# A gather-and-table transformer layer: eight more row pairs among the branch products, fourteen fewer ahead of the dense keys' weights, six of them in the last phase

## What is computed

```
h = layer_norm(x)
z = h @ W_in + b_in                       # 6400 columns: Fourier | q,k,v | memory q | gates
y_a, y_b, y_c = fourier(z) @ W_a, dilated_attention(z) @ W_b, memory_attention(z, mem) @ W_c
merged = sum_i sigmoid(gate_i) * y_i
h = layer_norm(alpha * h + merged @ W_o)
q = h @ W_pq                              # 8 heads, two halves each
s1, s2 = q1 . sub_keys1, q2 . sub_keys2   # 128 scores each
v1, i1, v2, i2 = top 16 of s1, top 16 of s2
sc, experts = top 16 of the 256 sums, expert = 128 * i1 + i2
gate = softmax(sc)
y = sum over 8 heads x 16 experts of gate * gelu(u_tab[expert] . h) * v_tab[expert]
out = layer_norm(alpha * h + y)
```

## Time and profile before

| | us |
|---|---|
| median of 3 runs | 1882.39 (1881.47 to 1882.58) |
| the profiled execution | 1882.71 |
| its span | 1880.9 |
| TensorE busy | 1710.1 (91%) |
| VectorE busy | 1250.8 (67%) |
| ScalarE busy | 204.6 (11%) |
| POOL busy | 635.2 (34%) |
| mean DMA rate | 263 GB/s |

### The profile page before, as it was taken

The page is one execution under the profiler, slowest core; times in us unless marked ns, Lnnn a source line. Parts: engine busy times, 40 slices in busy tenths (PEclk is TensorE's granted clock), DMA queues, the critical chain, the costliest instruction groups (busy, mean ns, idle before and its releaser), DMA issues.

```text
span 1880.9 us, 19525 instructions
## 1 busy us (share of the span) xinstructions
PE 1710.1 (91%) x7236; PEld 1213.9 (65%) x7236; DVE 1250.8 (67%) x2616; ACT 204.6 (11%) x431; POOL 635.2 (34%) x536
## 2 busy tenths in 40 slices
PE   7999999989999799999728899999999958799996
PEld 6588878967555668888527666666666547544442
DVE  3343175122567669997888986777777699966664
ACT  1101033101111021112100000111011010000000
POOL 2000000000246200146550175765665661265340
PEclk9999999999999989999867799999999976799998
DMA  6715201954779635679992199999999991299994
GB/s 221 235 45 158 83 7 40 286 166 145 243 266 370 246 124 175 217 261 409 388 356 62 51 400 409 409 409 409 397 409 409 409 372 61 77 404 410 409 403 151
DMA packets 193834, 493.81 MB, mean 263 GB/s; under 512 B 14103, under 2 KB 92952, under 8 KB 193444
## 3 DMA queue, kind: packets, MB, share of 16 engines
q0 software_dynamic: 74672, 271.55, 37.6%
q1 hardware_dynamic: 119068, 221.01, 33.1%
HBM read 489.32 MB, written 7.90 MB: 264 GB/s over the span
## 4 chain that ended last, share of the span: by engine, by line
PE 43%; DVE 26%; DMA 14%; POOL 9%; issue 7%; ACT 0%; SPq 0%; DVEq 0%
PE ps L639 42%; DMA arena<-in_v_tab_dram,experts 10%; POOL arena L604 5%; DVE arena L1336 5%; POOL arena L613 4%; DVE arena L1303 2%; DVE arena L1314 2%; DMA arena<-in_v_tab_dram 2%; DVE i L1233 2%; DVE pos L1248 1%; DVE arena L1302 1%; DVE v L1232 1%; DVE best L1247 1%; PE ps L651 1%; DMA arena<-in_w_mem_kv_dram 1%
## 5 line engine op out<-in xcount | busy, mean ns | idle before, releaser
L639 PE MATMUL ps<-arena 128*128 128x256 f32 (+4 forms) x6016 | 1503.1, 412 | 75.8 <-ACT arena L887 23.1
L639 PEld LDWEIGHTS ps<-arena 128*128 128x128 f32 (+1 forms) x6016 | 1035.9, 188 | 537.9 <-issue 285.9
L604 POOL DMA_INDIRECT arena<-in_u_tab_dram,experts x256 | 326.6, 1276 | 860.5 <-DVE dots L1314 531.6
L1336 DVE SCALAR_TENSOR_TENSOR arena<-arena,coef 128x1024 f32<-128x1024 f32 x254 | 327.3, 1289 | 111.0 <-DMA arena<-in_v_tab_dram,experts 110.2
L1314 DVE CUSTOM_DVE_ANT_0 arena<-arena 128x1024 f32<-128x1024 f32 x256 | 312.4, 1224 | 87.9 <-DMA arena<-in_u_tab_dram,experts 87.7
L613 POOL DMA_INDIRECT arena<-in_v_tab_dram,experts x256 | 297.3, 1161 | 148.3 <-DVE arena L1336 97.7
L887 ACT ACTIVATE arena<-ps 128x256 f32<-128x256 f32 (+2 forms) x212 | 88.9, 427 | 765.7 <-PE ps L639 722.0
L639 PE MATMUL ps<-hotg,arena 128*128 128x64 f16 x512 | 68.1, 303 | 26.8 <-DVE hotg L1304 25.5
L639 PEld LDWEIGHTS ps<-hotg,arena 128*128 128x128 f16 x512 | 59.9, 147 | 34.7 <-DVE hotg L1304 34.7
L1198 DVE TENSOR_TENSOR arena<-arena,ps 128x128 f32<-128x128 f32 (+1 forms) x32 | 13.4, 418 | 103.0 <-PE ps L639 91.7
L887 ACT ACTIVATE arena<-ps,bT 128x128 f32<-128x128 f32 (+2 forms) x68 | 36.6, 538 | 313.5 <-PE ps L639 313.5
(11 more groups left out here) (127 smaller groups left out, 793.3 us busy)
## 6 DMA issues: line engine op xcount, KB each, us to landing
arena<-in_u_cols_dram SPq DMA_DIRECT2D x128, 512.0 KB, 6.8
arena<-in_v_tab_dram SPq DMA_DIRECT2D x128, 512.0 KB, 6.8
arena<-in_w_in_dram SPq DMA_DIRECT2D x37, 1024.0 KB, 5.6
arena<-in_w_o_dram SPq DMA_DIRECT2D x8, 1024.0 KB, 9.9
arena<-in_w_pq_dram SPq DMA_DIRECT2D x8, 1024.0 KB, 5.4
beta_copies<-beta_rows SPq DMA_DIRECT2D x1, 4608.0 KB
arena<-in_w_mem_kv_dram SPq DMA_DIRECT2D x4, 1024.0 KB, 18.6
arena<-in_w_a_dram SPq DMA_DIRECT2D x8, 512.0 KB, 6.2
```

The costliest lines, as they stand in the source:

```text
L604: nc.gpsimd.indirect_dma_start(out=u_ring[:, n % ROWS, :], out_offset=None, in_=u_tab[0], in_offset=bass.IndirectOffsetOnAxis(ap=experts[: ...
L639: return nc.tensor.matmul(dst, lhsT, rhs, start=start, stop=stop, skip_group_check=True)
L1336: nc.vector.scalar_tensor_tensor(out=y_acc, in0=row, scalar=by, in1=y_acc, op0=ALU.mult, op1=ALU.add).then_inc(v_used, 1)
```

## The change

Two lines of constants change; V_PAIRS[1] follows from them and goes from 65 to 71.

```diff
-YO_PAIRS, TAIL_PAIRS = 36, 40
+YO_PAIRS, TAIL_PAIRS = 44, 48
 TOP_PAIRS = 8
-REST_PAIRS = 42
+REST_PAIRS = 28
 X_PAIRS = (4, 4)
 V_PAIRS = (118, PAIRS_IN - TAIL_PAIRS - TOP_PAIRS - REST_PAIRS - sum(X_PAIRS) - 118)
```

## The result

The changed kernel takes 1857.28 us (median of 4 runs, 1854.1 to 1860.1) against 1882.08 us before on the same chip: a ratio of 0.9868, 95% interval 0.9847 to 0.9889. Forecast were 1859.0 and a range of 1846 to 1872. Run once more beside other kernels it took 1855.16, a ratio of 0.9853 (0.9836 to 0.9869).

What follows compares the result with a forecast made beforehand. Bounds: TensorE in the tail and last phase, VectorE and its gathers ahead of the shares, VectorE at the first table phase's end. +10.6 - 46 + 0 + 7 + 5 = -23.4 us gave 1859.0 us, range 1846 to 1872.

Steps and rivals of the forecast that it cites:

- What bounds each stage: Second tail and last phase: TensorE; ahead of the shares: VectorE and its gathers; first table phase's end: TensorE waits for VectorE.
- Tail, +10.6: Second tail: three pairs and a head's key search before the last branch product start the output product 10.6 us later.
- crowded tail: Rival, second tail: rows wait, unit 22 is late, output product starts near 622; +8 more, 1867 us; chance 0.12.
- TensorE waiting for weights before 599: Second tail: sign that would show the prediction wrong; it took no wait for weights there.
- The clock: TensorE after the tail's wait: a 15 us wait costs the same 2 us or so as the present one; nothing added.
- 2 us more: TensorE at the shares: if the 33 us wait vanished wholly, the clock would give back some 2 us more.
- Ahead of the shares, -46: Before the dense keys' softmax shares: fourteen fewer pairs let VectorE reach them at 933 to 935, not 981.25; -46 us.
- 926: Dense keys on TensorE: key 59 could be emptied at 725.90 + 58 x 3.45 = 926.0, before the tail's delay.
- HBM rate: Ahead of the shares: measured 393 GB/s decides over the skill's about 358, which would leave the change worth about 4 us.
- Spreading phases, +10 and -10: Two spreading phases: one key search enters the first, another leaves the second; +10 and -10, together 0.
- First table phase, +7: First table phase: its last key search stands seven pairs before the end instead of thirteen; +7 us, bounds 0 and +8.3.
- Last phase, +5: Last phase: six more pairs at 4.03 us use up and overdraw VectorE's 18 us of cover; +5 us, bounds 0 and +9.

Runs made afterwards that it cites:

- tail_only: Against the kernel before: only YO_PAIRS, TAIL_PAIRS raised from 36, 40 to 44, 48, REST_PAIRS left at 42; 1899.54 us, ratio 1.0081.
- rest_only: Against the kernel before: only REST_PAIRS cut from 42 to 28, tail as before, all fourteen pairs going to the last phase; 1863.21 us, ratio 0.9900.
- change_again: The changed kernel run once more, nothing altered, beside the other kernels on one chip; 1855.16 us, ratio 0.9853.
- top38_late: Against the changed kernel: YO_PAIRS, TAIL_PAIRS, REST_PAIRS 41, 47, 29, putting one head's key search behind the last branch product; 1850.13 us, ratio 0.9818.

## Why the prediction was right, point by point

- **What bounds each stage.** Right at all four places of the kernel before. tail_only and rest_only, which move only one end each, changed the stages that the sums named by 8 us and more, and the others by 2.3 us at most. For the changed kernel the reading was wrong at one place, ahead of the shares (below).
- **Tail, +10.6.** The mechanism was right: units 22 and 23 are 16.44 us apart, 10.65 more than before, which is the sum of the added pair and top. The size was low by 1.5 to 4.7 us, because the term took no wait for weights or rows: in this profile TensorE lost 4.23 us on weights, in change_again unit 22 came 1.5 us later than before (597.90 against 596.45), without waiting for TensorE. The text had this as the rival "crowded tail" with a chance of 0.12; in part it came true, and so did one of the signs that I had named for being wrong, TensorE waiting for weights before 599. top38_late tells the two causes apart: with the top moved, 5.7 us of waiting remained beyond the 4.48 us of before, with 4.8 us of waits for rows on VectorE.
- **The clock.** After 15.13 us of waiting the clock was 0.50, as after 33.04 us; after 4.48 us it was 0.57. A longer wait did cost more than the short one, if little: the output product's 192 matmuls took 43.36 us behind 4.48 us of waiting and 44.52 behind 15.13 (44.12 in change_again), so the term that I left at nothing was some 1 us. The other half, that a wait which vanishes gives something back, also held. The four keys behind the transposes took 12.48 us instead of 13.83; before they were this:

```profile
983.79 13.83 PE L639 MATMUL ps<-arena 128*128 128x256 f32 x64
```

  These 1.35 us, and 0.67 in the transposes ahead of them (955.12 - 954.46 against 983.79 - 982.46), are the "2 us more" that the prediction gave by the Trainium skill (TensorE: Matmul & The Clock Gate, "Part 1: The HAM clock gate"); they are part of the +6.3 in the stage behind the transposes, which I had put at +10. The two fit together: +8.3 for the top and -2.0 for the clock.
- **Ahead of the shares, -46.** VectorE needed 45.2 us less from the output product to the shares (981.25 - 603.47 = 377.8, now 951.35 - 618.80 = 332.6). TensorE used 43.3 of them, since it now reached the transposes last. I had seen that limit but put it too early: with the tail's delay 926 would be 941, and it was 954. ScalarE emptied key 1 at 742.59 and key 59 at 954.66, 212.1 us apart, where the prediction counted 58 x 3.45 = 200.1. The timeline has six waits for table loads among the keys, 5.0 us together (the last is the 0.71 us above); the other 7 us I have not resolved. That VectorE's own end, 933 to 935 in the prediction, was right to 1 us (951.35 less the tail's 15.3 is 936) and that TensorE came only 3 us behind it is why this error does not show in the sum: it was luck. rest_only, where VectorE is 8 us earlier than TensorE, gives 330.1 us for this stage.
- **HBM rate.** The stretch with all keys and rows together ran at 404 GB/s over 443 us. The figure of some 358 GB/s that the Trainium skill states (DMA: Bandwidth & Descriptors, "Specifications") does not hold for this kernel on its one core, as the prediction had taken from the row of before.
- **Spreading phases, +10 and -10.** The wait for a top moved from the second to the first phase, 10.79 us there. The second phase gained only 8.3, the duration of the top itself: part of the 10.80 us was waiting that the phase has anyway, 2.5 us at each of the other pairs.
- **First table phase, +7.** The step was right in kind and too high in size: +3.4 (+3.0 in change_again). The kernels give a series by the number of pairs between the last top and the end: 468.9 us with 15, 468.7 and 470.4 with 13, 471.5 to 472.1 with 7, 477.3 with 5. The last, tail_only, also has an eighth top in the phase, so it does not belong to the series without question. Hardly any of a top's lag is left after thirteen pairs, and more of it is gone after seven than I had counted.
- **TensorE in that phase.** It needed 443 us instead of 454 and then waits 29.53 us for VectorE instead of 15.23. The 11 us bring nothing, since the pairs set the end. Why TensorE lost less inside the phase I have not tested.
- **Last phase, +5.** +3.9, and no idle time left ahead of the residual. rest_only adds the next point, 28.6 us for eight further pairs, 3.6 each, just under the 4.03 used.

The sum was right to 2 us (-23.4 forecast, -24.8 by the medians, -22.6 by the profiled executions) in part by luck, because errors of both signs met. Worse than forecast were the tail by 2 to 5 us, the stretch ahead of the shares by 1 to 3 and the second spreading phase by 2; better were the first spreading phase by 4, the first table phase by 4 and the last phase by 1 to 2.

## What to carry to other kernels

When work is moved between stages, walk the moved engine's queue at each stage's last dependency: what costs is what stands between the last two results that the next engine needs, not the stage's total. Rare long items (here a top of 8.3 us among pairs of 2.4 us) move with their numbers; place them where another engine covers them, and not within the last few items before a handover. A pair is free only while its stage has cover: count the cover in us, and stop when it is used.

## What the runs showed that I had not expected

The added gathers fall into a stretch that was already near a full DMA (395 GB/s between 575 and 600, before and after). TensorE then waits for a 1 MB load of gate weights in each of the four profiles with 44 pairs there, by 4.23, 3.38, 2.91 and 0.49 us, and in none of those with 41 or fewer. What decides it is how long one load takes to land, the 1 MB load issued between 560 and 575. It took 17.1, 16.2, 15.7 and 13.3 us in those four, in the same order, 11.1 to 11.7 in the four kernels with 38 or 41 pairs, and 5.2 to 5.3 in the two with 36. Landing less wait is some 12.8 us in each of the four: so much ahead of its use is the load issued, where the prediction took 14.2. With 38 it is the output weights that come last (5.43 us). The waits for gate weights differ between executions of one program, so they belong into a range and not into a sum.
